# Layer norm sums of the convolution branch: the eight channel tiles added on VectorE, then one matmul for each sum

## The reference, cut to what matters

```python
def layer_norm(x, g, b):
    xf = x.astype(jnp.float32)
    mu = jnp.mean(xf, axis=-1, keepdims=True)
    var = jnp.mean(jnp.square(xf - mu), axis=-1, keepdims=True)
    y = (xf - mu) * lax.rsqrt(var + EPS)
    return (y * g.astype(jnp.float32) + b.astype(jnp.float32)).astype(x.dtype)

# in each layer
u = causal_depthwise_conv(a_half * jax.nn.sigmoid(b_half), conv_b_w[layer]) + conv_b_b[layer]
y_b = jax.nn.silu(layer_norm(u, ln_b_g[layer], ln_b_b[layer])) * jax.nn.silu(z_b)
...
merged = (g_a * (y_a @ w_proj_a[layer]) + g_b * (y_b @ w_proj_b[layer])
          + g_c * (y_c @ w_proj_c[layer]))
x = x + gate * (merged @ w_out[layer])
```

## Time and profile before

| | |
|---|---|
| median of 3 runs | 2370.93 us |
| lowest, highest | 2368.96, 2371.85 us |
| the profiled execution, its own time | 2374.78 us |
| its span in the profile | 2373.0 us |
| mean granted TensorE clock | 0.974 |
| PE busy | 2261.2 us, 95% of the span |
| DVE busy | 1154.1 us, 49% |
| ACT busy | 953.3 us, 40% |
| POOL busy | 1660.5 us, 70% |

### The profile page before, as it was taken

The page is one execution under the profiler, slowest core; times in us unless marked ns, Lnnn a source line. Parts: engine busy times, 40 slices in busy tenths (PEclk is TensorE's granted clock), DMA queues, the critical chain, the costliest instruction groups (busy, mean ns, idle before and its releaser), DMA issues.

```text
span 2373.0 us, 40279 instructions
## 1 busy us (share of the span) xinstructions
PE 2261.2 (95%) x16408; PEld 2039.9 (86%) x16408; DVE 1154.1 (49%) x1682; ACT 953.3 (40%) x1037; POOL 1660.5 (70%) x676
## 2 busy tenths in 40 slices
PE   4799899999999999999998999999999999999999
PEld 3799899987779978787998999998777898788899
DVE  5849774845443353443533894664544335421110
ACT  3234344472332544343324444446433244443442
POOL 1468668765554798887767886876656458888876
PEclk8789999999999999999998999999999999999999
DMA  9967546544443598888856674554444337976664
GB/s 371 386 201 225 152 126 177 153 142 132 135 130 98 172 326 315 296 314 312 291 197 187 190 216 144 168 167 134 147 132 129 115 116 260 331 246 184 202 209 155
DMA packets 228840, 479.65 MB, mean 202 GB/s; under 512 B 22080, under 2 KB 26304, under 8 KB 220128
## 3 DMA queue, kind: packets, MB, share of 16 engines
q1 hardware_dynamic: 227392, 475.50, 62.3%
q10 hardware_dynamic: 1312, 2.23, 0.3%
HBM read 471.25 MB, written 6.29 MB: 201 GB/s over the span
## 4 chain that ended last, share of the span: by engine, by line
POOL 49%; issue 39%; PE 11%; POOLq 1%; DMA 0%; DVE 0%; ACT 0%; DVEq 0%; ACTq 0%
POOL wl L525 49%; PE ps L907 4%; PE ps L908 4%; PE ps L909 4%; POOLq L524 1%; PE ps L1331 0%; DMA raw<-w_in 0%; PE ps L996 0%; POOLq L520 0%; DVE xs L1978 0%; DVE ps L1705 0%; ACT wh L546 0%; ACT gate L534 0%; POOLq L525 0%; DVEq L1371 0%
## 5 line engine op out<-in xcount | busy, mean ns | idle before, releaser
L525 POOL TENSOR_TENSOR wl<-raw,wh 128x1024 fp32r<-128x1024 f32 x672 | 1660.3, 2483 | 699.4 <-ACT wh L546 698.1
L546 ACT CAST wh<-raw 128x1024 fp32r<-128x1024 f32 x672 | 701.5, 1049 | 1241.2 <-PE ps L909 973.6
L907 PE MATMUL ps<-ah,wh 128*128 128x256 f32 x3008 | 873.5, 290 | 53.4 <-DVE al L1478 27.3
L908 PE MATMUL ps<-al,wh 128*128 128x256 f32 x3008 | 859.7, 286 | 0.0
L909 PE MATMUL ps<-ah,wl 128*128 128x256 f32 x3008 | 859.4, 286 | 0.0
L907 PEld LDWEIGHTS ps<-ah,wh 128*128 128x128 f32 x3008 | 586.3, 195 | 62.0 <-DVE al L1478 27.6
L908 PEld LDWEIGHTS ps<-al,wh 128*128 128x128 f32 x3008 | 586.5, 195 | 4.7 <-issue 4.3
L909 PEld LDWEIGHTS ps<-ah,wl 128*128 128x128 f32 x3008 | 586.0, 195 | 0.0
L907 PE MATMUL ps<-wh,ah 128*128 128x512 f32 (+1 forms) x832 | 327.2, 393 | 1.0 <-POOL wl L525 0.9
L908 PE MATMUL ps<-wl,ah 128*128 128x512 f32 (+1 forms) x832 | 319.3, 384 | 0.0
L909 PE MATMUL ps<-wh,al 128*128 128x512 f32 (+1 forms) x832 | 319.3, 384 | 0.0
(11 more groups left out here) (259 smaller groups left out, 1840.6 us busy)
## 6 DMA issues: line engine op xcount, KB each, us to landing
raw<-w_in SPq DMA_DIRECT2D x512, 512.0 KB, 3.6
modw<-w_ada SPq DMA_DIRECT2D x64, 1024.0 KB, 7.8
adaw<-w_ada SPq DMA_DIRECT2D x64, 512.0 KB, 8.7
raw<-w_out SPq DMA_DIRECT2D x64, 512.0 KB, 4.4
raw<-w_pc SPq DMA_DIRECT2D x32, 512.0 KB, 3.7
raw<-w_pb SPq DMA_DIRECT2D x32, 512.0 KB, 7.0
raw<-w_pa SPq DMA_DIRECT2D x32, 512.0 KB, 4.5
gbias<-b_gate SPq DMA_DIRECT2D x24, 256.0 KB, 4.6
```

What stands on the lines that cost most here:

```text
L525: nc.gpsimd.tensor_tensor(wl[:, s], raw[:, s], wh[:, s].bitcast(F32), ALU.subtract).then_inc(sem("w_split"), 1)
L546: A.copy(wh[:, s], raw[:, s]).then_inc(sem("w_rounded"), 1)
L907: M.matmul(o, lh, rh, start=start, stop=False, skip_group_check=True)
L908: M.matmul(o, lh, rr, start=False, stop=False, skip_group_check=True)
```

## The change

Nothing else in the kernel moves. The sum over the eight tiles is taken over from PE by one `tensor_reduce` on DVE for each sum, into the new buffer `lss` (`[128, 2, 256]`, at 172 KB); one matmul with the ones then adds over partitions. The reduce reads its input with the tile index innermost (`"p c t -> p t c"`): 256 groups of eight numbers that lie 256 numbers (1 KB) apart. The first reduce is done in prep turn 2 through the hook `between`, behind level 1, and gives a new semaphore `ln_tiles` for which PE waits in `ln_sum`. The second stands behind `scan_v(2)`, with a drain in front of it; `ln_sq`, on which `ln_var` waits, now comes from it and no longer from the last squares. A layer of the changed kernel has 14 matmuls of source less and two reduces and one drain more.

```diff
@@ -239,6 +239,7 @@
         lnt = sb("lnt", 122, [CT, T])
+        lss = sb("lss", 172, [2, T])
@@ -1240,15 +1241,12 @@
                 def ln_sum():
                     pe.wait_ge(sem("inv_u"), 6 * 4 * L1)
                     pe.wait_ge(sem("prep_wT"), 4 * L1 + 1)
-                    for kt in range(CT):
-                        mm = M.matmul(pb[3][:, 0:T], ones, ub[:, kt], start=kt == 0, stop=kt == CT - 1)
-                    mm.then_inc(sem("ln_sum"), 1)
+                    pe.wait_ge(sem("ln_tiles"), L1)
+                    M.matmul(pb[3][:, 0:T], ones, lss[:, 0], start=True, stop=True).then_inc(sem("ln_sum"), 1)
 
                 def ln_var():
                     pe.wait_ge(sem("ln_sq"), L1)
-                    for kt in range(CT):
-                        mm = M.matmul(pb[3][:, T:2 * T], ones, lnt[:, kt], start=kt == 0, stop=kt == CT - 1)
-                    mm.then_inc(sem("ln_var"), 1)
+                    M.matmul(pb[3][:, T:2 * T], ones, lss[:, 1], start=True, stop=True).then_inc(sem("ln_var"), 1)
@@ -1816,6 +1814,12 @@
+                def ln_tiles(n):
+
+                    if n == 0:
+                        V.tensor_reduce(lss[:, 0], ub[:].rearrange("p c t -> p t c"), AX.X, ALU.add
+                                        ).then_inc(sem("ln_tiles"), 1)
+
@@ -1836,7 +1840,7 @@
                 for i in range(4):
-                    prep_turn(i, split_yc if i == 0 else None)
+                    prep_turn(i, split_yc if i == 0 else ln_tiles if i == 2 else None)
                     if i < 3:
                         prep_inputs(i + 1)
@@ -1877,8 +1881,11 @@
                 scan_s(1)
-                V.tensor_tensor(lnt[:, 4:8], ub[:, 4:8], ub[:, 4:8], ALU.mult).then_inc(sem("ln_sq"), 1)
+                V.tensor_tensor(lnt[:, 4:8], ub[:, 4:8], ub[:, 4:8], ALU.mult)
                 scan_v(2)
+                V.drain()
+                V.tensor_reduce(lss[:, 1], lnt[:].rearrange("p c t -> p t c"), AX.X, ALU.add
+                                ).then_inc(sem("ln_sq"), 1)
                 z_silu(2, 0, zs[1])
```

## The result

The changed kernel takes 2356.15 us (median of 14 runs, 2346.25 to 2361.84), the kernel before, run beside it, 2370.43 us (14 runs, 2364.41 to 2380.67). The ratio is 0.9938 [0.9926, 0.9950], that is 14.7 us less [11.9, 17.5]. The forecast was 2359.5, its range 2356.5 to 2365.5. The sign and the main mechanism were right; the forecast gain was 11.4 us where 14.7 were measured, and the time lies 0.35 us outside the range, far less than the uncertainty of the gain. The profiled execution took 2356.58 us.

A forecast was written before the change was run, and what follows sets the result against it. PE was taken to bound the kernel, busy 95% of the span. Four sums at 2.86 us less each, 11.4 us, with reduces and waits at nothing, took the median 2370.93 to 2359.5 us; range 2356.5 to 2365.5.

The forecast's parts named there:

- PE bounds, and what is taken from its list is gained: Around the scans PE is busy 54.00 of 54.00 us; shortening its list shortens the stretch, 11.4 us in all.
- The size of the term of the sum: Each sum on PE: 14 of 16 instructions go at 0.204 us, 2.86 us; four sums give 11.4 us.
- Rival 4: At the sums, a lone matmul exposes its start and end; PE keeps half of 3.27 us: 2365.2 us, chance 0.04.
- All moves together: Behind the sums, weight releases hang on PE; the later stage starts earlier and lasts as long, no further gain.
- The reduce: Each DVE reduce of 2048 elements takes 2.3 us by the softmax rows; high end 12.5 us.
- the slack of 4.2 us: In prep turn 2 the first reduce may last 4.2 us before PE waits; each us beyond costs PE one us.
- Second place: Second reduce, behind `scan_v(2)`, fits DVE's 5.16 us wait for ACT's tanh; even 7 us delays nothing.
- `scan_o(0)`, `lst`: Behind the first sum, `scan_o(0)` starts at 718.60, `vnew` in time by 0.8 us; `lst` at about 718.9 instead of 720.23.
- the waits on PE: PE's added wait for `ln_tiles` at the first sum costs nothing; even 0.1 us each is 0.2 us in all.
- Rivals 1 and 2: Long turn-2 reduce holds PE: at 7.0 us 2365.1 us, chance 0.10; at 12.5 us slower, 2379.1 us, chance 0.03.
- rival 2: Reduces at 12.5 us hold PE in turn 2 and the scan: 2379.1 us; slower from 9.9 us on; chance 0.03.
- Rival 3: Gain eaten in the later stage where PE waits 11.4 us for POOL: 2362.4 to 2368.1 us, chance 0.08.

The follow-up runs named there:

- e3: Kernel before with only tile 0 summed in both sums, one matmul each, no reduce: 2355.08 us, ratio 0.9941.
- e2: Changed kernel with the sums' eight matmuls each put back on PE, reduces kept but unread: 2370.43 us, ratio 1.0002.
- e5: Kernel before with both sums formed twice, 16 matmuls each: 2381.54 us, ratio 1.0044.
- e10: Kernel before with only the first sum (the mean's) formed twice, 16 matmuls: 2377.55 us, ratio 1.0038.
- e12: Kernel before with nine matmuls instead of eight in each sum: 2371.63 us, ratio 1.0000.
- e4: Changed kernel with only the first sum changed; the variance's keeps eight matmuls and has no reduce: 2359.44 us, ratio 0.9960.
- e7: Changed kernel plus six unread reduces at the end of layer 1, with varied element steps and group counts; single execution, 1 KB step 3.90 us.
- e6: Changed kernel with the reduce of prep turn 2 done twice: 2367.90 us, ratio 0.9986 to the kernel before.
- e8: Changed kernel with three quarters of layer 1's sum of squares also reduced on DVE first, one matmul each: 2353.63 us, ratio 0.9927 to the kernel before.
- e1: Changed kernel measured again as it is: 2356.73 us, ratio 0.9937 to the kernel before.
- e11: Changed kernel measured a third time as it is: 2352.54 us, ratio 0.9934 to the kernel before.

## Why the prediction was right and where it was wrong

- **PE bounds, and what is taken from its list is gained**: right, in the scans to the hundredth (PE busy 48.00 of 48.00 us), and e3 and e2 divide it as forecast: all of it in the matmuls, nothing in the reduces.
- **The size of the term of the sum**: a step that failed, too small. The prediction divided the 3.27 us by sixteen, and 14 x 0.204 = 2.86 us left a remaining pair at 0.41 us. But 3.27 is fifteen distances of 0.216 us and one of 0.03 to the next product, so fourteen instructions are 3.02 us, the pair costs 0.24, and four sums give 12.1 us instead of 11.4. e5, e10 and e12 agree: an instruction more costs 0.216 us as well. The trace of the kernel before had this distance. Rival 4 (a lone matmul exposes its ends) was wrong in sign, and its price too: by its own words, half of 3.27 instead of 0.41, it is 1.2 us a sum and 2364.4 us, not 2365.2.
- **"All moves together", so that the later stage "starts earlier and lasts as long"**: the step that failed by the most, a term put at nothing. Nothing was lost there that can be told, but the stage from 1926 to 2000 is 2.0 us shorter: PE's waits for POOL of 3.0 to 3.2 us became 1.5. The prediction asked of later waits only whether a gain could be lost in them, and not whether they could go; the 6.7 us of waits behind 1871 did not enter it. Its "no timer is in it" left out what the trace shows there, an issue of SP that ends with a packet of the instruction queue. Whether that is the cause, and why e4 keeps most of the wait, stays open.
- **The sum** made anew: 2359.5, less 0.5 us since three runs of before gave 2370.93 and fourteen give 2370.43, less 0.7 for the sums, less 2.0 behind the scan: 2356.3 us, measured 2356.15. That they meet so closely is luck, since the measured gain is known to 2.8 us either way.
- **The reduce**: 3.82 and 3.88 us, not 2.3. The Trainium skill's rule that the prediction set against the rows ("Vector Engine (DVE) Microarchitecture Reference", section "Measured stream behaviour on trn2") gave an estimated 3.7 for a hop at every element, and e7 agrees: 1.81 ns an element for a step of 1 KB, where the page lists 1.73 for a hop at every element. For a short step it lists some 2.5 ns; the step of 128 bytes took 4.03 us here, an estimated 1.9 ns. The measurement differs from the page for the step of 8 bytes: its elements aren't adjacent, and it ran at the full rate (2.27 us). Nearest row by operation and count was the wrong choice; what counted was the pattern of addresses. The error cost nothing, since the slack of 4.2 us was still larger. That is in part luck: the value chosen was 1.5 us too low, and only 0.4 us of the slack were left.
- **Second place, `scan_o(0)`, `lst`, the waits on PE**: right, each as the rows of the section on the result show.
- **Rivals 1 and 2**: not met, but e6 shows their price was wrong. "Each us beyond costs PE one us" left the clock out: 3.04 us of waiting cost 5.9 and 4.7 us. With that price rival 2 would begin not at a reduce of 9.9 us but not far above the 7.53 us of e6, where 5.3 us a layer are lost and the kernel is still 3.3 us below the one before (ratio up to 1.0000).
- **Rival 3**: not met, since the measured gain is more than all of what the sums give. The sign named for it, waits of 11.4 us that stay or grow, was no sign: their total was 6.2 to 11.4 us with PE's old list and 6.9 to 9.7 in the changed kernel. In e8 a part of a gain is eaten in this way.
- **The range**: its low end allowed 3 us below the forecast. The spread of before's three runs (2.9 us) stood for that of the kernel; seventeen runs in one batch spread over 10 us, and the changed kernel's fourteen over 15.6. The range left the upper side 6 us for rivals and the lower side nothing for waits that vanish. (The chances for "faster" are 0.90 by their parts, not 0.88.) The four comparisons of the full removal (the result, e1, e11, e3) give 14.0 to 15.6 us by their ratios.

## What to carry to other kernels

When the bound engine is nearly full, price removed instructions by the distance between neighbours in their run, and not by the run's length over their number, since the step to what follows can be far shorter. Ask of every later stage in which the bound engine waits both questions, whether the waits can grow and whether they can go, and widen the range downwards by the latter. Take a second profile of the same kernel before a total of waits is used as a sign: here it varied between 6.2 and 11.4 us by itself. An operation of unknown cost may be put into a measured wait when the slack is larger than its likely cost, but what lay beyond the slack here cost 1.5 to 1.9 times its length, since the clock fell behind the wait.

## What the runs showed of the hardware

- A float32 matmul of 256 columns shows as two instructions. In a row the instructions stood 0.216 us apart, and the next product started 0.03 us behind the last: 3.27 us for sixteen, 0.24 for two. Sixteen more cost 3.45 us, two more 0.43.
- A reduce's time on VectorE depended on the step between its elements: 1 KB 3.90, 128 bytes 4.03, 8 bytes 2.27, adjacent 2.26 us for 2048 elements; 8 or 256 groups made no difference (e7, one execution).
- A wait of TensorE of 3.0 us in a full stretch was followed by work at a granted clock of 0.50, in one layer for 6.1 us and in the other for 3.4, which cost 2.9 and 1.7 us on top of the wait.
- Two issues of 1 MB loads by SyncE took 0.88 us, or 1.6 to 1.7 us in the three profiles in which the first one met a 16 KB packet of the instruction queue; it ended 0.38 to 0.39 us behind that packet.
- The stage with the turn between the layers differed by 6.1 us between two profiles of the kernel before, and by 4.3 us between two of the changed one.
